# Ending each stage token half by token half, and ordering the first products of a stage by term

## What is computed

```python
def swiglu(u, w_gate, w_up, w_down):
    return (jax.nn.silu(u @ w_gate) * (u @ w_up)) @ w_down
...
def adaln_sublayer(x, m, f, ln_g, ln_b):
    shift, scale, gate = m[:, None, 0], m[:, None, 1], m[:, None, 2]
    y = f(x * (1 + scale) + shift)
    return layer_norm(DEEPNORM_ALPHA * x + (1 + gate) * y, ln_g, ln_b)
```

## Time and profile before

| what | value |
|---|---|
| median of 3 runs | 1687.15 us (1685.45 to 1691.71) |
| profiled execution, its own time | 1687.78 us |
| its span, first to last instruction | 1685.8 us |
| mean granted TensorE clock | 0.931 of 2.4 GHz |
| PE busy | 1483.1 us (88%), 8719 matmuls |
| DVE busy | 1170.0 us (69%) |
| ACT busy | 865.0 us (51%) |
| DMA | 306.46 MB, 182 GB/s over the span |

### The profile page before, as it was taken

One profiled execution on the slowest core, in us unless ns is written; L12 is line 12 of the kernel. 1 busy time (PEld: TensorE's weight loads), 2 busy tenths in 40 slices (PEclk: granted clock), 3 DMA queues, 4 the chain that ended last, 5 costly groups with the idle time before them and its releaser, 6 DMA issues.

```text
span 1685.8 us, 23219 instructions
## 1 busy us (share of the span) xinstructions
PE 1483.1 (88%) x8719; PEld 1262.5 (75%) x8719; DVE 1170.0 (69%) x2090; ACT 865.0 (51%) x1591; POOL 0.2 (0%) x4
## 2 busy tenths in 40 slices
PE   2999989897979999899998668899996997799987
PEld 2888879786757888688886555688885994599745
DVE  5888879858568887788888446686668345454364
ACT  1555454542445544554555347455555965485463
POOL 0000000000000000000000000000000000000000
PEclk9999999998979999899999789899997998899887
DMA  9898868530036897479793160385564450546000
GB/s 368 303 326 319 291 198 262 175 101 1 1 100 226 314 321 258 142 260 339 274 312 113 46 226 3 122 291 197 186 199 138 150 179 1 150 117 211 26 1 25
DMA packets 197515, 306.46 MB, mean 182 GB/s; under 512 B 10562, under 2 KB 159132, under 8 KB 197404
## 3 DMA queue, kind: packets, MB, share of 16 engines
q1 hardware_dynamic: 195744, 303.55, 53.0%
q10 hardware_dynamic: 1660, 1.43, 0.3%
HBM read 303.91 MB, written 1.05 MB: 181 GB/s over the span
## 4 chain that ended last, share of the span: by engine, by line
PE 72%; DVE 12%; ACT 5%; issue 2%; PEld 1%; DMA 1%; ACTq 0%; PEldq 0%; DVEq 0%
PE bank L853 17%; PE bank L780 12%; PE bank L782 11%; PE bank L781 11%; PE bank L852 8%; PE bank L1318 2%; PE bank L1290 2%; PE bank L1303 1%; DVE wp_lo L1088 1%; PE bank L855 1%; PE bank L372 1%; DVE w_lo L903 1%; ACT arena L1353 1%; DVE uT L574 1%; DVE x_tok L578 1%
## 5 line engine op out<-in xcount | busy, mean ns | idle before, releaser
L853 PE MATMUL bank<-u_hi_lo,w_hi 128*128 128x512 f32 x1408 | 502.7, 401 | 12.6 <-DVE u_hi_lo L448 5.2
L852 PE MATMUL bank<-u_hi_lo,w_lo 128*128 128x256 f32 x1232 | 349.1, 283 | 1.4 <-DVE u_hi_lo L448 1.4
L903 DVE TENSOR_TENSOR w_lo<-weight_ring,w_hi 128x1024 fp32r<-128x1024 f32 x264 | 307.9, 1220 | 12.6 <-ACT w_hi L873 12.0
L853 PEld LDWEIGHTS bank<-u_hi_lo,w_hi 128*128 128x128 f32 x1408 | 262.2, 191 | 66.5 <-issue 6.3
L873 ACT CAST w_hi<-weight_ring 128x1024 fp32r<-128x1024 f32 x264 | 260.2, 1046 | 8.5 <-PE bank L782 5.6
L852 PEld LDWEIGHTS bank<-u_hi_lo,w_lo 128*128 128x128 f32 x1232 | 235.7, 191 | 14.9 <-DVE u_hi_lo L448 6.9
L1088 DVE TENSOR_TENSOR wp_lo<-weight_ring,wp_hi 128x1024 fp32r<-128x1024 f32 (+4 forms) x149 | 167.5, 1165 | 56.7 <-ACT wp_hi L1055 56.4
L780 PE MATMUL bank<-src_hi,wp_hi 128*128 128x256 f32 (+1 forms) x632 | 190.4, 301 | 4.9 <-DVE src_lo L448 4.8
L781 PE MATMUL bank<-src_lo,wp_hi 128*128 128x256 f32 (+1 forms) x632 | 182.3, 288 | 0.0
L782 PE MATMUL bank<-src_hi,wp_lo 128*128 128x256 f32 (+1 forms) x632 | 182.1, 288 | 0.0
L1055 ACT CAST wp_hi<-weight_ring 128x1024 fp32r<-128x1024 f32 (+4 forms) x149 | 143.6, 1007 | 63.5 <-PE bank L782 57.6
(11 more groups left out here) (351 smaller groups left out, 2171.0 us busy)
## 6 DMA issues: line engine op xcount, KB each, us to landing
weight_ring<-in_mod_w_dram SPq DMA_DIRECT2D x72, 1024.0 KB, 6.7
weight_ring<-in_ffn_w_gate_dram SPq DMA_DIRECT2D x44, 1024.0 KB, 5.5
weight_ring<-in_ffn_w_up_dram SPq DMA_DIRECT2D x44, 1024.0 KB, 5.4
weight_ring<-in_ffn_w_down_dram SPq DMA_DIRECT2D x44, 1024.0 KB, 8.1
weight_ring<-in_hyb_w_in_dram SPq DMA_DIRECT2D x16, 1024.0 KB, 8.5
weight_ring<-in_w_in_e_dram SPq DMA_DIRECT2D x16, 1024.0 KB, 5.4
weight_ring<-in_w_in_o_dram SPq DMA_DIRECT2D x13, 1024.0 KB, 5.3
weight_ring<-in_hyb_w_out_dram SPq DMA_DIRECT2D x4, 1024.0 KB, 4.8
```

What stands on the lines that cost most here:

```text
L852: nc.tensor.matmul(bank[:, 0:SEQ], w[1], u[:, 0:SEQ], start=False, stop=False, skip_group_check=True)
L853: last = nc.tensor.matmul(bank[:, :], w[0], u, start=kt == 0, stop=kt == KT - 1, skip_group_check=True)
L903: nc.vector.tensor_tensor(part_view(wl, n, part), raw, part_view(wh, n, part).bitcast(F32), ALU.subtract).then_inc(w_lo.sem, w_lo.up())
```

## The change

1. **Token half 1 is put off and added in two column blocks.** In `ffn`, for the last four hidden tiles (18 to 21) a step makes only token half 0 of the down product; half 1 of tile 18 is made in step 21, and that of tiles 19 to 21 behind the last step, first column block 0, then block 1. Hidden buffers go from 3 to 4, weight slots in `ffn` from 6 to 8. In `out_proj`, token half 1 of the last two of four jobs is made behind all jobs, block by block. A new signal `tokens_out` is raised after each block.
2. **The heads follow.** `early` on DVE adds token half 0 whole and block 0 of half 1; block 1 is added after `stage_done`. The row sum of half 1 is made of two partial sums. `early_act` is new: ACT loads its table and does `spread(0)` (or `mean_square(0)`) before `stage_done`. In `LayerNorm` DVE now norms all four quarters, and `spread(1)` comes between the two casts of the first weights. `RootMeanSquare` and `BothNorms` do `spread(1)` or `mean_square(1)` ahead of the casts.
3. **First products by term.** Step 0 of `ffn` and job 0 of the four mixers do first all hi·hi (waiting for `act_hi` of each c), then the terms with the weights' lo, then those with the source's lo (waiting for `act_lo` of each c). In `ffn` the 512-column matmuls of that step become two of 256 columns.
4. **`X_STEP`** goes from 20 to 18.

```diff
-            def add(self, dve, a):
-                dve.wait_ge(*self.y[a])
...
+            def summed(self, dve, a, cols, out):
+
+                dve.wait_ge(vstep.sem, vstep.count)
+                nc.vector.scalar_tensor_tensor(out=x_tok[:, a, cols], in0=x_tok[:, a, cols], scalar=ALPHA,
+                                               in1=self.t[:, a, cols], op0=ALU.mult, op1=ALU.add, accum_out=out) \
+                    .then_inc(z_ready.sem, z_ready.up())
...
+            def add_half(self, dve, h):
+
+                dve.wait_ge(*self.y[1 + h])
+                self.gated(dve, 1, h)
+                self.summed(dve, 1, half_row(h), col((S_SUM, S_HALF)[h], 1))
+                if h == 0:
+                    nc.vector.tensor_scalar(col(S_PART, 1), col(S_SUM, 1), -1.0 / DM, None, ALU.mult) \
+                        .then_inc(vstep.sem, vstep.up())
+                else:
+                    nc.vector.scalar_tensor_tensor(out=col(S_MEAN, 1), in0=col(S_HALF, 1), scalar=-1.0 / DM,
+                                                   in1=col(S_PART, 1), op0=ALU.mult, op1=ALU.add) \
+                        .then_inc(mean_ready.sem, mean_ready.up())
...
             def early(self, dve):
                 self.columns(dve)
-                self.add(dve, 0)
+                self.add_first(dve)
+                self.add_half(dve, 0)
+
+            def early_act(self, act):
+                nc.scalar.activation(warm[:, :], ones[:, 0:1], ACT.Sqrt)
+                self.spread(act, 0)
...
             def act(self, act, split_hi, hi):
-                nc.scalar.activation(warm[:, :], ones[:, 0:1], ACT.Sqrt)
-                split_hi(0)
-                for a in range(TT):
-                    self.spread(act, a)
-                self.centre_act(act, half_row(0)).then_inc(normed_act.sem, normed_act.up())
+                split_hi(0, 0)
+                self.spread(act, 1)
+                split_hi(0, 1)
...
             def dve(self, dve, split_lo, hi, lo):
-                self.add(dve, 1)
-                self.inverse(dve, 0, S_INV, S_SPREAD, 1)
-                for h in range(2):
-                    self.centre(0, half_row(h)).then_inc(normed_dve.sem, normed_dve.up())
-                self.inverse(dve, 1, S_INV, S_SPREAD, 2)
-                self.shift_col(dve, 1)
-                self.centre(1, half_row(1)).then_inc(normed_dve.sem, normed_dve.up())
+                self.add_half(dve, 1)
+                for a in range(TT):
+                    self.inverse(dve, a, S_INV, S_SPREAD, a + 1)
+                    for h in range(2):
+                        self.centre(a, half_row(h)).then_inc(normed_dve.sem, normed_dve.up())
                 split_lo(0)
...
+        FF_HALVES = 8
+        HELD = 4
...
-            X_STEP = FT - 2
+            X_STEP = FT - 4
...
+                def first_step():
+                    w = [(n, part_view(wh, n, part), part_view(wl, n, part)) for n, part, _, _, _ in steps[0]]
+                    for c in range(4):
+                        pe.wait_ge(act_hi.sem, act_hi.base + c + 1)
+                        for part, (n, hi, lo) in enumerate(w):
...
+                            for kt in (2 * c, 2 * c + 1):
+                                nc.tensor.matmul(PB[part][:, 0:SEQ], hi[:, kt, :], uh[:, kt, :], start=kt == 0,
+                                                 stop=False, skip_group_check=True)
+                    for part, (n, hi, lo) in enumerate(w):
+                        pe.wait_ge(w_lo.sem, w_lo.base + n + 1)
...
+                    for c in range(4):
+                        pe.wait_ge(act_lo.sem, act_lo.base + c + 1)
...
+                            late = jj >= FT - HELD
+                            for a in range(1 if late else TT):
                                 for h in range(2):
-                                    o = half_row(h)
-                                    last = product(y_bank(a, h), (hh[:, jj % 3, tok], hl[:, jj % 3, tok]),
-                                                   (hi[:, o], lo[:, o]), jj == 0, jj == FT - 1)
-                                if a == 0 and jj == FT - 1:
-                                    last.then_inc(y_first.sem, y_first.up())
+                                    last = down(jj, a, h)
                             last.then_inc(w_used.sem, w_used.up())
+                            if jj == FT - 2:
+                                for h in range(2):
+                                    down(FT - HELD, 1, h)
+                for h in range(2):
+                    for jj in range(FT - HELD + 1, FT):
+                        last = down(jj, 1, h)
+                    last.then_inc(tokens_out.sem, tokens_out.up())
...
+                def first_job():
+                    fill = jobs[0][3]
+                    for term in range(3):
+                        for n, ka, kb, tile in pieces[0]:
...
+            def tail(weights, sh, sl):
+
+                for h in range(2):
+                    for t in (2, 3):
+                        for k in range(2):
+                            last = part(t, k, 1, h, (sh[:, 2 * t + k, :], sl[:, 2 * t + k, :]), weights(t, k))
+                    last.then_inc(tokens_out.sem, tokens_out.up())
```

More of the change, by code:

```diff
@@ L651, in turns @@
                         self.turn(x, 0, c)
-                for h in range(2):
-                    if h:
-                        pe.wait_ge(normed_dve.sem, normed_dve.base + 3)
-                    else:
-                        pe.wait_ge(normed_act.sem, normed_act.base + 1)
+                for h, (ready, n) in enumerate(self.second):
+                    pe.wait_ge(ready.sem, ready.base + n)
                     for c in (2 * h, 2 * h + 1):
@@ L776, in two_blocks_kernel, with product, term_of @@
         src_turned = signal("projection_source_turned")
-        def product(out, lhs, rhs, start, stop, group=False):
-            nc.tensor.matmul(out, lhs[0], rhs[0], start=start, stop=False, skip_group_check=group)
-            nc.tensor.matmul(out, lhs[0], rhs[1], start=False, stop=False, skip_group_check=group)
-            return nc.tensor.matmul(out, lhs[1], rhs[0], start=False, stop=stop, skip_group_check=group)
+        HIGH_HIGH, HIGH_LOW, LOW_HIGH = (0, 0), (0, 1), (1, 0)
+        ALL_TERMS = (HIGH_HIGH, HIGH_LOW, LOW_HIGH)
+        WEIGHTS_FIRST = (HIGH_HIGH, LOW_HIGH, HIGH_LOW)
+        SOURCE_FIRST = (HIGH_HIGH, HIGH_LOW, LOW_HIGH)
+        def product(out, lhs, rhs, start, stop, group=False, terms=ALL_TERMS):
+            for i, (l, r) in enumerate(terms):
+                last = nc.tensor.matmul(out, lhs[l], rhs[r], start=start and i == 0, stop=stop and i == len(terms) - 1,
+                                        skip_group_check=group)
+            return last
+        def term_of(order, term):
+            return ALL_TERMS if term is None else (order[term],)
         silu_ready = signal("gate_silu_ready")
@@ L1047, in _, with split_hi @@
             def _(act):
+                if head is not None:
+                    head.early_act(act)
                 act.wait_ge(stage_done.sem, stage_done.base)
-                def split_hi(j):
-                    for n, ka, kb, tile in pieces[j]:
+                def split_hi(j, one=None):
+                    for n, ka, kb, tile in pieces[j] if one is None else pieces[j][one:one + 1]:
                         act.wait_ge(loaded[tile.slot], tile.need)
@@ L1159, in proj_T, with fill @@
             nt_n = n // P
-            def fill(bank, wt, kt, src):
+            def fill(bank, wt, kt, src, term=None):
                 for nt in range(nt_n):
@@ L1164, in fill @@
                                    (wt[0][:, nt * P:(nt + 1) * P], wt[1][:, nt * P:(nt + 1) * P]),
-                                   src, kt == 0 and nt == 0, kt == k - 1, group=True)
+                                   src, kt == 0 and nt == 0 and not term, kt == k - 1 and term in (None, 2), group=True,
+                                   terms=term_of(WEIGHTS_FIRST, term))
                 return last
```

182 lines of the change are left out of this document (118 added, 64 removed).

## The result

| | before | after |
|---|---|---|
| median, first comparison | 1687.07 us (4 runs) | 1671.88 us (4 runs, 1668.48 to 1673.56) |
| median, repeated | 1689.17 us (9 runs) | 1668.99 us (4 runs, 1668.41 to 1669.36) |
| ratio | | 0.9907 [0.9889, 0.9925], then 0.9882 [0.9868, 0.9895] |
| profiled execution, its span | 1687.78, 1685.8 us | 1668.48, 1666.5 us |
| granted clock | 0.931 | 0.939 |

So the change makes the kernel 0.9% to 1.2% faster, 15 to 20 us. The forecast was 16.4 us, 1671.

The account below looks back on a forecast made before the run. The prediction took DVE's chain to bound the stage starts, with PE waiting for it. Gains at the starts and the last additions, net of clock costs, summed to 16.4 us, from 1687.8 to 1671 us, range 1661 to 1681.

Parts of the forecast that it names:

- DVE sets the starts: At the seven stage starts, 17.1 to 30.4 us each, PE waits for DVE, which is busy 85% to 95%.
- Part 1 and 2: Stage 1 to 2: half sum 0.74 us, mean of half 1 at T+1.7 (T: stage's last product), `low` 2.1 earlier.
- Part 3, stage 1 to 2: Products by term: step 1 at T+17.35 (T: stage's last product) after 3.4 us idle; net gain of this start 1.3.
- shortens nothing here: Stage 1 to 2: order by term leaves PE idle 3.4 us before step 1, paying 1.8 us one step later.
- What the idle costs: Behind 3.4 us of PE idle before step 1, the clock at 1.2 GHz loses 1.7 us, ends 0 and 3.4.
- no clock cost: Rival, chance 0.2: the clock level stays high over the idle, 6.6 us come back, 1664 to 1665 us.
- Stage 3 to 4: DVE's way between sums grows to 10.15 us, stage 3 ends 3.1 later; net gain at the start of stage 4 0.35.
- once: Stage 3: PE would wait about 1.8 us for DVE's L914 a single time.
- The mixers: Starts of stages 1, 6 and 7, where PE does not wait for a bank: gains of 2.75, 4.5 and 2.9 us.
- Last additions: End of the last stage: one add instead of two left after the last product, 0.65 us gained.
- Only the early adding pays: Rival, chance 0.22: order by term finds PE bound by DVE in mixers too; gain 8.5 us, 1679 us.
- The lower clock stays: Rival, chance 0.04: a doubled low stretch, 12.2 us, at all seven starts loses 43 us, giving 1707 us.

Follow-up runs that it names:

- the filled idle: Twelve unused 512-column matmuls put behind step 0 of each feed-forward stage of the changed kernel; 1660.97 us, ratio 0.9847.

## Why the prediction was right, step by step

**DVE sets the starts: shown for the feed-forward stages.** Taking the early adding away brings the whole time back; changing only DVE's order in them gives 7 to 10 us more; changing only PE's order in them gives nothing. In the mixers PE's order counts as well: without it their second jobs begin 6.0 us later in all. (The least busy start of the earlier trace rows has DVE at 84%, 14.52 of 17.30, and not at 85%; nothing hangs on it.)

**Part 1 and 2.** The half sum was taken as 0.74 and took 0.69 (495.65 above). The Trainium skill (VectorE: DVE Perf Modes, the TRN2 errata) gave the estimate 0.69, and the trace agrees with it. The mean stands at T+1.75 (forecast T+1.7). `low` ended at T+12.8 to T+13.4 in the stages that were forecast at T+13.05 to T+13.65, so the terms were 0.2 us too careful.

**Part 3, stage 1 to 2.** Step 1 at T+17.2 (17.35), idle 3.00 (3.4), step 2 at T+27.2 (25.75 and 1.7 for the clock, 27.45). Net 1.6 against 1.3. That the order by term "shortens nothing here" was tested alone and holds, 1669.81 against 1668.99. The 1.8 us that it was to pay in step 1 is eaten by the lower clock, which it moves from step 0 into step 1.

**What the idle costs.** 1.7 per start was forecast, 1.6 to 2.7 measured in stages 2, 3 and 5. The rival "no clock cost" falls by the stretch at 0.66 and by the filled idle. The prediction's evidence was thinner than it reads: at two of its three places, 3.48 and 3.02 us idle, the level was low already before the idle (from 1645.0 and from 941.8 us). An idle of 3.00 us in stage 5 of the run with the order by term alone had full clock behind it, and so had one of 2.02 us in stage 0 of the changed kernel repeated. The cost is what mostly happens, not a rule. The Trainium skill's section on HAM oscillation (TensorE: Matmul & The Clock Gate) holds here in kind at stages 2, 3 and 5 of the kernel after (0.66 over the 5 us behind the idle of stage 2): idle, then a burst that begins at the lower clock.

**Stage 3 to 4.** DVE's way between the sums was forecast at 10.15 us and took 10.15 (873.19 to 883.34). The sign "once" was wrong: PE waited twice, 1.39 and 1.63 us. That is not where the time went, for the sum had the cost of the end nearly right: stage 3 wins 2.3 us up to step 2 (T+28.1 against T+30.4) and is 1.0 to 1.2 longer, so its end costs 3.4 instead of the 3.1 forecast. The other part of the miss is the start, 2.3 instead of 2.7: the clock took 2.7 and not 1.7 there, and `low` ended 0.2 earlier than forecast. Stage 4 gave back what was forecast. Stage 0's end was put at nothing and cost 0.7: there too DVE sums modulation vectors in the last steps, and PE, whose step is shorter by the half that is put off, waits 0.72 us for L967 before step 20.

**The mixers.** Stage 1: 2.9 to 3.3 against 2.75. Stage 6: 4.4 to 5.9 against 4.9. Read at the marks of the tables the starts were 3.1, 3.8, 6.0 and 3.2 us shorter where the sum had 2.75, 3.45, 4.9 and 2.9: each term was right in kind, and that of stage 6 was 1.1 too small. Before, the first job of stage 6 ran at a clock of 0.63 (from 1294.1 to 1302.6); after, the transposes run at the lower level and the first job at the full one:

```profile
1277.90:1281.30 3.40, 3.40 (x17) 3.18 (x17) 2.94 (x5) 2.33 (x7) 0.00 (x0) 0.53 0.92 285
1281.30:1288.60 7.30, 6.83 (x49) 5.99 (x48) 7.16 (x14) 6.00 (x11) 0.00 (x0) 1.00 0.53 158
```

**Last additions.** One of 0.69 us after the last product, as forecast:

```profile
1663.38 0.69 DVE L3181 TENSOR_TENSOR x_tok<-x_tok,bank 128x512 f32<-128x512 f32 x1 [2.03 <-PE bank L827]
```

**How exact the hit is.** The terms erred both ways. The starts were 2.4 us better than forecast (the mixers by 2.1, the feed-forward stages by 0.3), the ends of stages 0 and 3 1.0 worse. That makes about 18 us where the sum had 16.4, in one profiled execution; the medians say 15.2 and 20.2. The sum is right in its parts, but that it lands within 1 to 2 us of either median is partly luck, since the comparisons themselves differ by 5 us in what the change is worth.

**The rivals.** "Only the early adding pays" (1679) is half true: the early adding carries 13.6 us, more than the 8.5 worked out for it, and order by term adds 2 to 5 us by the medians (3 to 7 by the ratios), all of it in the mixers, where this rival had it worth nothing. "The lower clock stays" did not happen: in the kernel after, the low stretch behind step 1's idle ended within 5.3 us each time.

## What to carry to other kernels

Find the engine whose written-out order sets a start, and put the operation that frees the other engine's buffer ahead of work that is needed only later. Reordering the other engine's work without that only moves its idle time, and an idle of 3 us was paid once more by the clock behind it in most places here. Work that can be held back until one half of the data is finished is worth most when the half that is finished starts a long chain (13.6 us here); check what it frees at the end, since PE then waited for DVE there.

## What was not expected of the hardware

- A clock loss is free where another engine sets the pace: 3.1 us lost in step 0 and 1.7 us lost in step 1 gave the same start of step 2, T+27.2.
- Twelve useless matmuls, 2.93 us, made the kernel 8 to 11 us faster, though PE's work grew.
- The level of the clock in one stretch of unchanged work differs from execution to execution: 0.74 or 0.82 over the last attention, 4 us. Over the rest of the mixers' unchanged work two executions differ by 7.6. Such differences hide a change of this size in a single stage, and why the level differs is open.
